# Order of the work in the first block's heads, and GpSimd's mask minus bias in sixteen instructions

## The reference

```
# first block, one layer
proj = rms_norm(x, ln1) @ w_in
y_moba  = softmax(causal(q k^T / 8)) v            # 6 heads of 64, q and k normed and rotated
y_mlstm = rms_norm(mlstm(q, k, v, gates) * sigmoid(xo))   # 4 heads
y_swa   = softmax with sink, window 128           # 6 query heads, 2 key heads
x = x + concat(y_moba, y_mlstm, y_swa) @ w_out
x = x + relu(rms_norm(x, ln2) @ w_up)**2 @ w_down
# second block, one layer
x = x + 0.5 * swiglu(...)
o_na = neighbourhood attention, 8 heads: where(mask, s + rpb, -1e30)
o_sw = sliding window attention, 8 heads, bias and sink
x = x + (g0 * (o_na @ w_na) + g1 * (o_sw @ w_sw)) @ w_out
x = x + 0.5 * swiglu(...)
```

## Time and profile before

| | us |
|---|---|
| median of 3 runs | 1711.79 (1710.69 to 1712.68) |
| the profiled run | 1713.88 |
| its span, first to last instruction | 1712.1 |
| TensorE busy | 1676.2 |
| DVE busy | 1245.1 |
| ACT busy | 994.0 |
| GpSimd busy | 166.4 |
| mean granted clock of TensorE | 0.997 |

### The profile page before, as it was taken

The page is one execution under the profiler, slowest core; times in us unless marked ns, Lnnn a source line. Parts: engine busy times, 40 slices in busy tenths (PEclk is TensorE's granted clock), DMA queues, the critical chain, the costliest instruction groups (busy, mean ns, idle before and its releaser), DMA issues.

```text
span 1712.1 us, 25589 instructions
## 1 busy us (share of the span) xinstructions
PE 1676.2 (98%) x9966; PEld 1452.1 (85%) x9966; DVE 1245.1 (73%) x1985; ACT 994.0 (58%) x1664; POOL 166.4 (10%) x116
## 2 busy tenths in 40 slices
PE   7989999998999999999999999999999999999999
PEld 5778888877888888888778988888888787898888
DVE  7777766767776567876776878767786767778874
ACT  5666654566665455554477655545554457765552
POOL 2611000161200000000321000000000221000000
PEclk9999999999999999999999999999999999999999
DMA  7525555542655645556433555555555543445553
GB/s 289 187 99 185 197 192 202 212 145 99 229 182 205 209 181 190 196 197 247 173 121 123 176 194 189 191 205 193 184 195 205 213 178 118 148 173 197 188 203 127
DMA packets 62022, 313.98 MB, mean 183 GB/s; under 512 B 22685, under 2 KB 24353, under 8 KB 25294
## 3 DMA queue, kind: packets, MB, share of 16 engines
q1 hardware_dynamic: 60382, 303.93, 50.0%
q0 software_dynamic: 1232, 4.22, 0.8%
q10 hardware_dynamic: 288, 4.19, 0.7%
HBM read 311.25 MB, written 7.36 MB: 186 GB/s over the span
## 4 chain that ended last, share of the span: by engine, by line
PE 89%; DVE 6%; ACT 4%; issue 1%; DMA 0%; SPq 0%; DVEq 0%; ACTq 0%
PE acc L411 45%; PE acc L413 23%; PE acc L400 4%; PE acc L402 4%; PE acc L401 4%; DVE w_lo L386 3%; ACT w_hi L377 1%; PE acc L420 1%; PE acc L422 1%; PE acc L421 1%; PE acc L810 1%; PE tp L796 1%; PE sc L785 1%; PE tp L931 1%; PE sc L915 1%
## 5 line engine op out<-in xcount | busy, mean ns | idle before, releaser
L386 DVE TENSOR_TENSOR w_lo<-raw,w_hi 128x1024 fp32r<-128x1024 f32 (+1 forms) x564 | 692.5, 1235 | 275.2 <-ACT w_hi L377 273.5
L377 ACT ACTIVATE w_hi<-raw 128x1024 fp32r<-128x1024 f32 (+1 forms) x564 | 583.6, 1038 | 198.2 <-PE acc L413 120.7
L411 PE MATMUL acc<-act_a,w_hi 128*128 128x512 f32 x1440 | 505.5, 395 | 1.2 <-DVE w_lo L386 1.2
L411 PE MATMUL acc<-hidden,w_hi 128*128 128x512 f32 x1216 | 421.8, 392 | 0.0
L413 PE MATMUL acc<-act_a,w_lo 128*128 128x256 f32 x1440 | 402.7, 280 | 0.0
L413 PE MATMUL acc<-hidden,w_lo 128*128 128x256 f32 x1216 | 339.8, 279 | 0.0
L411 PEld LDWEIGHTS acc<-act_a,w_hi 128*128 128x128 f32 x1440 | 269.7, 187 | 69.1 <-issue 9.2
L413 PEld LDWEIGHTS acc<-act_a,w_lo 128*128 128x128 f32 x1440 | 272.1, 189 | 0.1
L411 PEld LDWEIGHTS acc<-hidden,w_hi 128*128 128x128 f32 x1216 | 227.5, 187 | 50.4
L585 ACT COPY part<-acc 128x256 f32<-128x256 f32 x272 | 101.0, 371 | 282.7 <-PE acc L413 281.6
L411 PE MATMUL acc<-act_b,w_hi 128*128 128x512 f32 x688 | 239.5, 392 | 0.0
(11 more groups left out here) (217 smaller groups left out, 2038.7 us busy)
## 6 DMA issues: line engine op xcount, KB each, us to landing
raw<-in_slabs SPq DMA_DIRECT2D x282, 1024.0 KB, 4.8
na_skew<-in_rpb SPq DMA_DIRECT2D x32, 128.0 KB
na_bias<-na_skew ACTq DMA_DIRECT2D x2, 2048.0 KB, 8.2
t_skew<-t_by_distance POOLq DMA_DIRECT2D x2, 1024.0 KB, 14.1
t_bias<-t_skew POOLq DMA_DIRECT2D x1, 2048.0 KB, 10.9
x_res<-in_x SPq DMA_DIRECT2D x1, 1024.0 KB, 4.9
out_x<-x_res SPq DMA_DIRECT2D x8, 128.0 KB, 4.9
prow<-in_prow SPq DMA_DIRECT2D x1, 518.0 KB
```

The source lines that it names most:

```text
L377: nc.scalar.activation(w_hi[u % RING][:, 0:n], raw[j % RAW][:, (u % 2) * HALF:(u % 2) * HALF + n], ACT.Copy).then_inc(s["unit_hi"], 1)
L386: nc.vector.tensor_tensor(w_lo[u % RING][:, 0:n], raw[j % RAW][:, (u % 2) * HALF:(u % 2) * HALF + n], w_hi[u % RING][:, 0:n].bitcast(F32), ...
L411: nc.tensor.matmul(bank[:, :], wh, src[:, c + i, :, :].rearrange("p i s -> p (i s)"), start=first and i == 0, stop=False, skip_group_check ...
```

## The change

In the first block's heads, with i the loop's counter:

- DVE: `seconds(i + 2)` moves in front of `first(i + 4)` and of the low part of y.
- TensorE: for i > 4, `values(i - 2)` moves in front of `scores(i + 4)`. The y turn moves from before output chunk 1 to behind it, in the same round; the chunks stay in theirs.
- Splits: ACT makes unit 4 at i = 4 (was 2), unit 5 at 8 (was 4), 6 at 10 (was 6), 7 at 12 (was 8), 8 at 14 (was 12); DVE unit 4 at i = 6 (was 4), 5 at 10 (was 6), 6 and 7 at 12 (were 8 and 10), 8 at 14 (was behind the loop).
- `y_first` and `y_mean` stay at i = 4 and 6; only their names are new.

On GpSimd, mask minus bias becomes sixteen instructions of 128 x 256 in place of one of 128 x 4096, and each gate product two of 128 x 256 in place of one of 128 x 512.

```diff
-        SWA_TURN, Y_TURN = 2, LSTM + MOBA
+        SWA_TURN, Y_TURN = 2, 10
+        OUT_FIRST = LSTM + MOBA - 2
+        Y_SEEN, Y_MEAN = 4, 6
+
+        SPLIT_ACT = {0: 4, 4: 5, 8: 6, 10: 7, 12: 8, 14: 9}
+        SPLIT_DVE = {2: 4, 6: 5, 10: 6, 12: 8, 14: 9}
...
-                if i + PROBS < N1:
+                if i <= LSTM and i + PROBS < N1:
                     scores(i + PROBS)
                 if i >= 2:
                     values(i - 2)
+                if i > LSTM and i + PROBS < N1:
+                    scores(i + PROBS)
...
+                if OUT_FIRST <= i <= OUT_FIRST + 4:
+                    out_chunk((i - OUT_FIRST) // 2)
                 if i == Y_TURN:
                     wait(pe, value(b, "y_ready", 1))
                     turn_tiles(f["y"], lstm_h, 0)
-                if Y_TURN - 2 <= i <= Y_TURN + 2:
-                    out_chunk((i - Y_TURN) // 2 + 1)
...
-                if i < Y_TURN:
-                    act_split(act, b, u0 + RING + i // 2)
-                if i == Y_TURN + 2:
-                    act_split(act, b, u0 + RING + Y_TURN // 2)
+                if i in SPLIT_ACT:
+                    act_split(act, b, u0 + SPLIT_ACT[i])
...
-            act_split(act, b, u0 + RING + Y_TURN // 2 + 1)
+            act_split(act, b, u0 + DC + 2)
...
+                if LSTM <= i + 2 < N1:
+                    seconds(i + 2)
                 if i + PROBS < N1:
                     first(i + PROBS)
                     first(i + PROBS + 1)
...
-                if LSTM <= i + 2 < N1:
-                    seconds(i + 2)
                 if i - 2 >= LSTM:
                     pair(i - 2)
-                if i <= Y_TURN:
-                    dve_split(dve, b, u0 + RING - 1 + i // 2)
-                if i == LSTM:
+                if i in SPLIT_DVE:
+                    dve_split(dve, b, u0 + SPLIT_DVE[i])
+                if i == Y_SEEN:
                     y_first()
-                if i == LSTM + 2:
+                if i == Y_MEAN:
                     y_mean()
-            dve_split(dve, b, u0 + RING + Y_TURN // 2 + 1)
+            dve_split(dve, b, u0 + DC + 2)
...
-            nc.gpsimd.tensor_tensor(nb, mask_n[:, :].unsqueeze(1).broadcast_to([P, T * NA, S]), nb, ALU.subtract)\
-                .then_inc(s["bias_ready"], 1)
+            for i in range(T * NA):
+                ins = nc.gpsimd.tensor_tensor(nb[:, i], mask_n[:, :], nb[:, i], ALU.subtract)
+            ins.then_inc(s["bias_ready"], 1)
...
-                nc.gpsimd.tensor_tensor(g2[:, n, :, :], g2[:, n, :, :], r_of(2), ALU.mult).then_inc(s["zg_ready"], 1)
+                for i in range(2):
+                    ins = nc.gpsimd.tensor_tensor(g2[:, n, i, :], g2[:, n, i, :], r_bc[:, :], ALU.mult)
+                ins.then_inc(s["zg_ready"], 1)
```

## The result

The changed kernel takes 1702.62 us (median of four runs, 1701.92 to 1703.1) beside 1712.24 for the kernel before on the same chip (1710.69 to 1712.86): ratio 0.994, 95% interval 0.9926 to 0.9953. That is 9.6 us less, 2.4 us more than the 1700.2 of the prediction and inside its range. The profiled run took 1703.1 with a span of 1701.3; against the span of 1712.1 before that is 10.8 us less.

What follows compares the result with a forecast made beforehand. TensorE, busy 98% of the span, was taken as the bound, so only its stops could be won. Mask -8.3 and heads -3.8 make -12.1 us from the 1711.79 median: 1699.7, rounded up to 1700.2, range 1696.5 to 1705.5.

Steps and rivals of the forecast that it cites:

- Mask, -8.3: Second block's mask, both layers: sixteen pieces let DVE's split in, so TensorE's stop and the clock's fall go, -8.3 us.
- Rival C: At the mask, GpSimd's sixteen pieces run without letting DVE in, holding `w_lo` 11.8 us: slower, 1717.0 us; chance 0.05.
- the 5 us of cover: At the mask: the later result, ready at about 830, stays hidden before GpSimd's next work at 835.5, 5 us to spare.
- Heads, layer one, -1.2: First block's heads, layer one: TensorE's stops sum to 5.7 us in place of 6.85, -1.2 us (+0.5 to -2.5).
- The three small ones: Layer one's heads: stops of 0.44 us at divisions(10), 0.3 before scores 14, 0.2 at chunk 2 for unit 5.
- One sign of being right: In the first block's heads, no division pair would take over 1.1 us next to GpSimd.
- Heads, layer two, -2.6: First block's heads, layer two: stops 5.3 us for 6.2, and the clock's fall of 1.7 us gone, -2.6 us.
- rival A: The heads' stops, now spread, let the clock fall in one layer (1701.9 us) or both (1703.6); chance 0.27.
- B: Heads give nothing or lose: new stops each 0.5 us longer, clock falls in both layers, 1703.5 to 1706; chance 0.12.
- D: Mask does half: pieces hold the split up to 7 us, costing 1 to 2 us a layer, 1704 to 1709; chance 0.05.
- E: More than forecast: y and divisions come earlier, heads' stops under 3 us a layer, 1695 to 1697 us; chance 0.09.
- later splits catch up: Behind the heads: unit 9 split at 119.9, wanted at 125; slabs land by 118, wanted at 122; nothing lost.

Runs made afterwards that it cites:

- `divisions_first`: Kernel before with both GpSimd edits and, of the heads' moves, only DVE's divisions in front of maxima and of y's low part: 1701.16 us.
- `heads_alone`: Changed kernel with GpSimd's old mask and gate instructions, so only the new order in the first block's heads: 1709.39 us, ratio 0.9983.
- `scores_first_at_six`: Changed kernel with TensorE's scores in front of the values again at i = 6: 1699.27 us, run again 1699.07.
- the early mean: `scores_first_at_six` with y's mean of squares moved between divisions(8) and maxima(10) on DVE: 1701.53 us, ratio 0.9943.
- `gpsimd_alone`: Kernel before with only GpSimd's edits, mask minus bias in sixteen and gate products in two: 1705.62 us, ratio 0.9961.

## Why the prediction was right, and where its terms were off

**Mask, -8.3.** Right in mechanism: DVE's split gets in behind a piece (1.23 to 1.78 us in both layers; bound 1.24 + 0.74), no stop, no fall, ready at 827.0 where I said 830. Between the two profiles it is 8.1. Rival C, pieces one behind the other, did not happen. What was off is the step "the clock falls behind that pause" taken as certain: the price was read from one execution that held both falls, while a fall costs 1.5 and comes in some executions only. Median against median the term is 6.8 to 7.3. Two side readings were off without a price: DVE first reads the result at 859.9, not 863, and the 5 us of cover before GpSimd's next work at 835.5 left out that this work comes earlier by the gain itself; 1.9 were left.

**Heads, layer one, -1.2.** Measured -1.53. The walk named every stop that came, with its size: 0.76 where I had 0.9 (heads), 0.75 for 0.8 (V's eviction), 0.65 for 0.6 (unit 4), 1.67 for 1.8 (y_lo), 0.57 at scores 6, unchanged (these are idle times of the rows, 0.1 to 0.2 us under the count that the prediction uses). The three small ones (0.44, 0.3, 0.2) did not come at all. That is why more was gained. Counted alike, by the idle times in the rows, the stops went from 5.96 us (0.57 + 0.48 + 1.51 + 1.63 + 0.92 + 0.85) to 4.40, which is the -1.53 of the marks to 0.03. One sign of being right did not hold: the divisions of 8 take 2.60 us at 94.95 (1.01 before), as the new order puts them beside GpSimd's first products of y at 94.69 and 96.05. No stop of TensorE stands behind them. And `divisions_first` shows that the walk's moves on TensorE, which brought the new stops on V, unit 4 and y_lo, were not what won.

**Heads, layer two, -2.6.** Measured -0.91; this is the term that is farthest off. "The fall of the clock gone, as the 1.64 + 1.00 behind one another are gone" holds in `heads_alone`, where the stretch takes 123.38 us, 2.5 less than before, as forecast. It does not hold in the changed kernel's profile: same stops, and the clock falls at 412.2, +1.57. That is rival A, priced at 1.7 for one fall, in this one execution. It is not what made the time 1702.62 and not 1700.2: the three runs without a fall lie there too, only 0.4 to 1.2 us under the profiled 1703.1.

**Sum.** -8.1 for -8.3, -1.5 for -1.2, -0.9 for -2.6, and 0.2 at the start of the program: 10.8 in place of 12.1 of the span. And I set that difference against the median of 1711.79, though the profiled run of before, 1713.88, lay 2 us above it. This is the step that made the forecast 2.4 us too low: the 12.1 take three falls away, and most runs of the kernel before hold one. Two falls at the 1.36 us of the 45 runs are 2.7 us, and 9.4 in place of 12.1 stands beside the measured 9.6. The clocks of the runs behind the 1711.79 are not on record, so that these held one is taken over from the others. Without any fall on either side, four runs of before at a mean of 1709.7 against the three of the changed kernel at 1702.4, the change is worth 7.3; those were not taken side by side.

**Rivals B, D, E.** No new stop was 0.5 us longer than walked (B), no split at the mask over 1.8 us (D). E's stops of under 3 us a layer came only with `scores_first_at_six` (2.99), and at 1699.27, not at its 1695 to 1697.

**The faith in "later splits catch up"** was right for the slabs: nothing behind the heads grew, as the stretch of 361.31 us shows.

## What to carry to other kernels

A long GpSimd product or sum can hold whatever DVE issues next, small instructions too; cut it into pieces that are shorter than the slack of every DVE instruction queued there, and check that the engine's own next work can bear the longer total. A profile is one execution: before its falls of the clock are priced, compare its mean granted clock with those of the other runs, and take off a median only the falls that its own runs hold. The stop is certain, the clock behind it is not. In an order written out by hand a stop's named releaser is only the last link: moving it forward can put its producers onto another engine's work, as the early mean did, or push back what stood in front. So try the moves one at a time; here a single move won as much as all of them together, or more.

## What the runs showed of the hardware

- The same stops do and don't bring a fall of the granted clock: 0.65 and 1.68 us, 8.4 us apart, with a fall in the changed kernel and without one in `heads_alone`. A fall to the lower level of 1.2 GHz cost 1.1 us (layer two's heads, 125.86 in the kernel before against 124.73 in `gpsimd_alone`) to 1.6 us.
- Over 45 runs of the kernel before the time rises by 1.36 us for each 0.001 that the mean granted clock is lower, from 1709.0 us at 1.000 to 1716.9 at 0.995.
- Sixteen 128x256 subtractions on GpSimd take 17.18 us with DVE's splits between them, 9.01 as one instruction. A DVE split beside them takes 1.23 to 1.78 us in place of 1.22.
- A DVE `tensor_scalar` of 128x8 took 4.58 us beside a GpSimd instruction of 128x2048, 0.70 beside pieces of 128x256; an addition of 128x4 took 0.76 in place of 0.16 beside a GpSimd product of 128x512.
- Not every long GpSimd instruction holds DVE: beside the power at L2104 (128x32, 6.34 us from 828.86 in the changed kernel) DVE's two splits at 828.69 took 2.41 us together, as much as two alone.
